# Two-block transformer kernel, dense passes: tokens and accumulator in twos of 16-token runs, upper runs first, at three address distances

## The chip, the core and the metric

The kernel runs on one core of a Trainium2 chip. The metric is device time of one execution in microseconds (us). All data are on the core: weights come from HBM once, and the tokens (512 of them, 1024 features) stay in SBUF from the first load to the last store.

## The reference

`reference()` puts a sequence of 512 tokens through two blocks, in float32:

- `first_block`: a norm, one projection to 18 groups of 128 columns, four mixers (gated MLP over chunks, RG-LRU, HGRN2, pooling), an output projection, a convolutional feed-forward network of width 2816, and an embedding gate.
- `second_block`: two hybrid layers. Each has this core (shortened):

```python
h = _rms(x) * norm1_g
proj = h @ w_in
aq, ak, av, rw, rq, rk, rv, rg, gates = _split(proj, IN_SIZES)
o_a = sliding_window_attention(aq, ak, av, sinks) @ w_attn_o
o_b = rwkv7_time_mix(rw, ...) @ w_rwkv_o
o_c = retention(rq, rk, rv, rg) @ w_ret_o
g = jax.nn.sigmoid(gates).reshape(B, T, N_BRANCH, D)
x = x + (g[:, :, 0] * o_a + g[:, :, 1] * o_b + g[:, :, 2] * o_c) @ w_out
h2 = _rms(x) * norm2_g
x = x + (jax.nn.silu(h2 @ w_ffn_gate) * (h2 @ w_ffn_up)) @ w_ffn_down
```

Most of the arithmetic is in the dense products of the 512 tokens with weight matrices.

## The kernel before, in words

**Layout.** Features lie on the 128 partitions and tokens along the free dimension. A tile such as `xg_hi` has 8 chunks (`DC`) of 512 tokens (`T`), so one chunk is 2048 bytes per partition.

**Dense products.** A float32 value is split into a high part that fits the fp32r format and a low part, the rest. A product takes three matmuls per chunk: high weights by high tokens, high weights by low tokens, low weights by high tokens. This text calls one such matmul, 128 x 128 weights by 512 tokens into one accumulator bank, a *dense pass*. The weights are the operand that is loaded into the array (LDWEIGHTS, shown as PEld), the tokens the operand that is streamed through it.

**Slots.** A slot makes 128 output features: 8 chunks and so 24 passes (4 chunks and 12 passes for the output projections of the mixers, 6 and 18 for the last part of the feed-forward products, 2 and 6 for the embedding). Two slots alternate, with accumulators `acc[0]` and `acc[1]`, weight tiles `w_hi[:, s]`, `w_lo[:, s]` and the raw weights in `raw[:, s]`. For each slot

- SyncE loads 512 KB (or less) of raw weights when the slot before in the same place has been split,
- GpSimd makes the high part (line 369, when the high passes of the slot before are done) and the low part (line 376, when all its passes are done),
- TensorE runs the passes, through `slot`, `late`, `three`, `part` or `first_slots`, all by the helper `mm` at line 550,
- VectorE or ScalarE takes the accumulator away.

The tokens of a product are in one of these pairs of tiles: `xg` (normed tokens, for the input, gate, feed-forward-up and output-gate products), `hid` (hidden or mixed features), `y` (mixer outputs of the first block), `y1` and `y2` (mixer outputs of the layers, placed over `z_rw` and `z_rt`), `emb` (embedding). `an_hi` and `an_lo`, sums over attention queries in the same number format, use `mm` and are not among the dense passes here.

**Order of work.** Each engine has a program written out by hand, and semaphores join them. In the RWKV part of a layer TensorE runs a chain of small matmuls that depends on VectorE, ScalarE and GpSimd at each step. Between the steps the list `FILLS` puts dense passes of later slots, 96 for each of 4 pairs of heads, in each of the 2 layers. The retention and attention parts put whole slots between their steps.

**Addresses.** `place` hands out SBUF addresses. With `line=` an address is moved up until it is that number modulo `LINE`, 512 bytes. Before the change every token tile has START, 128, and by the same rule `raw`; `w_hi` and `w_lo` follow `raw` directly at multiples of 512 bytes, so they are at 128 as well. A weight tile of one pass is 128 x 4 = 512 bytes per partition.

Of the kernel before, what the change touches and what calls it, by code (L numbers as in the profile page):

```python
# [14 lines left out]
F32, F32R, U32 = mybir.dt.float32, mybir.dt.float32r, mybir.dt.uint32  # L15
# [3 lines left out]
P = 128  # L19
T = 512  # L20
NT = T // P
D = 1024
DC = D // P
# [5 lines left out]
EPS = 1e-6  # L29
LN_EPS = 64e-5  # L30
DECAY = float(np.exp(-0.5))
LINE, START = 512, 128


B1_IN, X_OUT, O_PAIRS, PE_PAIRS = 9, 4, 24, 8
# [71 lines left out]
def build(nc, dram, out):  # L107
    ctx = ExitStack()
    with ctx:
# [3 lines left out]
        def place(name, shape, dt=F32, offset=None, line=None):  # L113
            n = 4 * int(np.prod(shape))
            if offset is None:
                if line is not None:
                    at[0] += (line - at[0]) % LINE
                offset = at[0]
                at[0] += (n + 31) // 32 * 32
            return nc.alloc_sbuf_tensor_at(name, [P, *shape], dt, offset=offset), offset  # L120

        x, _ = place("x", (DC, T))
        xg_hi, _ = place("xg_hi", (DC, T), F32R, line=START)
        xg_lo, _ = place("xg_lo", (DC, T), F32R, line=START)
        junk, _ = place("junk", (1,))
        raw, _ = place("raw", (2, DC * P), line=START)
        w_hi, _ = place("w_hi", (2, DC * P), F32R)
        w_lo, _ = place("w_lo", (2, DC * P), F32R)
        rstd, _ = place("rstd", (T,))
# [4 lines left out]
        base = at[0]  # L134
# [2 lines left out]
        for name, shape in FIRST:  # L137
            K[name], _ = place(name, shape, U32 if name == "hgmask" else F32)
        z, _ = place("z", (18, T))
        y_hi, _ = place("y_hi", (DC, T), F32R, line=START)  # L140
        y_lo, _ = place("y_lo", (DC, T), F32R, line=START)
        m1 = {}
        for name, shape in (("ta", (2, T)), ("tb", (2, T)), ("tc", (2, T)), ("td", (2, T + 16)), ("te", (2, T)), ("tf", (2, T)),
                            ("tg", (2, T)), ("th", (2, T))):
# [17 lines left out]
        for name, shape in RETAT:  # L162
            K[name], _ = place(name, shape)
        at[0] = max(end, at[0])
        z_rw, rw_at = place("z_rw", (14, T), line=START)
        z_rt, rt_at = place("z_rt", (16, T))
        scratch = at[0]
        C4 = 4 * 4 * T
# [5 lines left out]
        y2_lo, _ = place("y2_lo", (4, T), F32R, offset=rt_at + C4)  # L174
        hid_hi, _ = place("hid_hi", (DC, T), F32R, offset=rt_at)
        hid_lo, _ = place("hid_lo", (DC, T), F32R, offset=rt_at + 2 * C4)
        emb_at = base + 24 * 1024 + (START - base) % LINE
        emb_hi, _ = place("emb_hi", (2, T), F32R, offset=emb_at)
        emb_lo, _ = place("emb_lo", (2, T), F32R, offset=emb_at + C4 // 2)
        emb, _ = place("emb", (2, T), F32, offset=emb_at + C4)  # L180
        assert {a % LINE for a in (rw_at, rt_at, emb_at)} == {START} and emb_at + 3 * C4 // 2 <= rt_at and base + 4 * sum(int(np.prod(shape)) for _, shape in FIRST) <= emb_at

        rw = {}
        for name, shape in (("kk", (T,)), ("sq", (T,)), ("kp", (T,)), ("a", (T,)), ("Lr", (T,)), ("Dl", (T,)), ("eM", (T,)),
# [355 lines left out]
        def _(pe):  # L540
# [4 lines left out]
            def columns_of(w, s, k):  # L545

                return w[:, s, k * P:(k + 1) * P]

            def mm(o, a, b, first, last, shared=False):
                return nc.tensor.matmul(o, a, b, start=first, stop=last, skip_group_check=shared)  # L550

            def slot(s, I, a, chunks, early=False, stat=None, to=None, free=None):

                hi, lo = a
                if early:
                    pe.wait_ge(w_half[s], I + 1)
                else:
                    pe.wait_ge(w_split[s], I + 2)
                if to is None:
                    pe.wait_ge(acc_free[s], I + 1 if free is None else free)  # L560
                pe.sem_inc(pe_turn, 1)
                n = len(chunks)
                o = acc[s] if to is None else to
                for m, v in ((0, hi), (0, lo), (1, hi)):
                    w = (w_hi, w_lo)[m]
                    if early and m == 1:
                        pe.wait_ge(w_split[s], I + 2)
                        pe.sem_inc(pe_turn, 1)
                    for k, c in enumerate(chunks):
                        last = mm(o[:], columns_of(w, s, k), v[:, c, :], v is hi and m == 0 and k == 0, m == 1 and k == n - 1)  # L570
                    if v is lo:
                        last.then_inc(hi_done[s], 1)
                        if stat is not None:
                            pe.wait_ge(keep_in, load_wait * len(keep_names))
                            stats(stat)
                last.then_inc(slot_done[s], 1)

            def late(s, I, a, chunks, ready, count, order=None, early=False, stat=None):

                pe.wait_ge(w_half[s], I + 1) if early else pe.wait_ge(w_split[s], I + 2)  # L580
                pe.wait_ge(acc_free[s], I + 1)
                pe.sem_inc(pe_turn, 1)
                n = len(chunks)
                if early:
                    for k, c in enumerate(chunks[:-1]):
                        pe.wait_ge(ready, count + k + 1)
                        pe.sem_inc(pe_turn, 1)
                        mm(acc[s][:], columns_of(w_hi, s, k), a[0][:, c, :], k == 0, False)
                        mm(acc[s][:], columns_of(w_hi, s, k), a[1][:, c, :], False, False)
                    pe.wait_ge(w_split[s], I + 2)  # L590
                    pe.sem_inc(pe_turn, 1)
                    for k, c in enumerate(chunks[:-1]):
                        mm(acc[s][:], columns_of(w_lo, s, k), a[0][:, c, :], False, False)
                    if stat is not None:
                        stats(stat)
                    pe.wait_ge(ready, count + n)
                    pe.sem_inc(pe_turn, 1)
                    k, c = n - 1, chunks[-1]
                    mm(acc[s][:], columns_of(w_hi, s, k), a[0][:, c, :], False, False)
                    mm(acc[s][:], columns_of(w_hi, s, k), a[1][:, c, :], False, False).then_inc(hi_done[s], 1)  # L600
                    mm(acc[s][:], columns_of(w_lo, s, k), a[0][:, c, :], False, True).then_inc(slot_done[s], 1)
                    return
                for i, k in enumerate(order or range(n)):
                    c = chunks[k]
                    pe.wait_ge(ready, count + i + 1)
                    pe.sem_inc(pe_turn, 1)
                    mm(acc[s][:], columns_of(w_hi, s, k), a[0][:, c, :], i == 0, False)
                    last_hi = mm(acc[s][:], columns_of(w_hi, s, k), a[1][:, c, :], False, False)
                    last = mm(acc[s][:], columns_of(w_lo, s, k), a[0][:, c, :], False, i == n - 1)
                last_hi.then_inc(hi_done[s], 1)  # L610
                last.then_inc(slot_done[s], 1)

# [6 lines left out]

            def three(s, a, k, first, last):  # L620

                mm(acc[s][:], columns_of(w_hi, s, k), a[0][:, k, :], first, False)
                hi_pass = mm(acc[s][:], columns_of(w_hi, s, k), a[1][:, k, :], False, False)
                return hi_pass, mm(acc[s][:], columns_of(w_lo, s, k), a[0][:, k, :], False, last)

            def hid_slots(I, n, count, ahead=0):
                if not ahead:
# [187 lines left out]
            pe.wait_ge(acc_free[0], I + 1)  # L815
            for c in full:
                w = columns_of(w_hi, 0, c)
                mm(acc[0][:], w, xg_hi[:, c, :], c == 0, False)
                last = mm(acc[0][:], w, xg_lo[:, c, :], False, False)
            last.then_inc(hi_done[0], 1)  # L820
            pe.wait_ge(w_split[0], I + 2)
            for c in full:
                last = mm(acc[0][:], columns_of(w_lo, 0, c), xg_hi[:, c, :], False, c == DC - 1)
                if c < DC - 1:
                    last.then_inc(xg_free, 1)
            last.then_inc(slot_done[0], 1)
# [2 lines left out]
            def first_slots(I):  # L829
# [1 line left out]
                early, rest = range(6), range(6, DC)  # L831

                def one(s, w, v, c, first=False, last=False):
                    return mm(acc[s][:], columns_of(w, s, c), v[:, c, :], first, last, True)

                def started(s):
                    pe.wait_ge(w_half[s], I + 1)
# [31 lines left out]
            for l in range(LAYERS):  # L869
# [7 lines left out]
                def part(s, I, lo, hi):  # L877

                    for k in range(lo, hi):
                        if k == 0:  # L880
                            pe.wait_ge(w_half[s], I + 1)
                            pe.sem_inc(pe_turn, 1)
                            pe.wait_ge(acc_free[s], I + 1)
                            pe.sem_inc(pe_turn, 1)
                        if k == 2 * DC:
                            pe.wait_ge(w_split[s], I + 2)
                            pe.sem_inc(pe_turn, 1)
                        w, v, c = (w_hi, w_hi, w_lo)[k // DC], (xg_hi, xg_lo, xg_hi)[k // DC], k % DC
                        last = mm(acc[s][:], columns_of(w, s, c), v[:, c, :], k == 0, k == 3 * DC - 1, True)
                        if k == 2 * DC - 1:  # L890
                            last.then_inc(hi_done[s], 1)
                        if k == 3 * DC - 1:
                            last.then_inc(slot_done[s], 1)
# [1849 lines left out]
```

## Time and profile before

| what | us |
|---|---|
| median of 3 runs | 2546.61 |
| lowest and highest run | 2546.43, 2551.27 |
| the profiled execution, its own time | 2548.05 |
| span of that execution, first to last instruction | 2546.2 |
| TensorE busy in it | 2511.3 |
| GpSimd busy in it | 1512.5 |
| VectorE busy in it | 1311.4 |
| ScalarE busy in it | 691.6 |

The durations quoted below come from the one profiled execution. Its own time is 1.8 us more than its span, which is what lies ahead of the first instruction and behind the last. In the profile PE is TensorE with its matmuls, PEld its weight loads, DVE VectorE, ACT ScalarE, POOL GpSimd and SP SyncE. A matmul's record runs from its start to its modelled end; since matmuls follow each other through the array, records of neighbours overlap, and from one start to the next is less time than one record lasts. L550 is line 550 of the kernel.

### The profile page before, as it was taken

Reading aid. Unit: us, or ns where it says so; the run is one execution under the profiler, and the core shown is the slowest. Engines: PE = TensorE matmul, PEld = TensorE weight load, DVE = VectorE, ACT = ScalarE, POOL = GpSimd, SP = SyncE. Lnnn points to the kernel's source line nnn. Section 1 sums busy time; section 2 is a strip of 40 time slices with the busy share of each in tenths; the row PEclk is TensorE's granted clock in tenths of the full one; section 3 lists DMA queues with packets and bytes.
Section 4 is the critical chain, followed back from the end, with each engine's and each line's share of the span. In section 5 each row is a group of like instructions: output and inputs, shape, how many; then the busy total and the mean of one; then the engine's idle time right before and its main releaser. Section 6 shows DMA issues by size and latency. Waiting matters only on the chain.

```text
span 2546.2 us, 47105 instructions
## 1 busy us (share of the span) xinstructions
PE 2511.3 (99%) x16344; PEld 2012.3 (79%) x16344; DVE 1311.4 (52%) x1979; ACT 691.6 (27%) x1290; POOL 1512.5 (59%) x963
## 2 busy tenths in 40 slices
PE   8989999999999999999999999999999999999999
PEld 6868888887877778888888888867678888888887
DVE  7867555465566657663322224566647663322224
ACT  4452000024135446521100002134446531100002
POOL 5666666656646455556666666645454556666665
PEclk9999999999999999999999999999999999999999
DMA  4213222223211122223222223211122223222223
GB/s 167 71 43 119 91 99 99 91 86 117 92 51 52 44 97 69 72 87 103 93 97 99 96 93 122 91 47 50 51 97 67 75 87 103 91 99 95 95 99 99
DMA packets 72442, 222.55 MB, mean 87 GB/s; under 512 B 9312, under 2 KB 12256, under 8 KB 72288
## 3 DMA queue, kind: packets, MB, share of 16 engines
q1 hardware_dynamic: 71856, 220.36, 26.3%
q8 instruction: 96, 1.57, 0.3%
q14 instruction: 58, 0.48, 0.1%
q10 hardware_dynamic: 432, 0.14, 0.0%
HBM read 218.37 MB, written 2.10 MB: 87 GB/s over the span
## 4 chain that ended last, share of the span: by engine, by line
PE 92%; DVE 4%; DVEq 1%; issue 1%; DMA 1%; POOL 1%; ACT 0%; ACTq 0%; POOLq 0%; SPq 0%
PE acc L550 80%; PE bank L550 10%; DMA raw<-in_w_pg 1%; PE bank L1214 0%; POOL w_lo L376 0%; DVE sumsq L1252 0%; DVE y_lo L1252 0%; DVE bank L1252 0%; DVE xg_lo L1345 0%; POOL w_hi L369 0%; DVE bank L1611 0%; DMA vec<-in_vec 0%; DVE att L1464 0%; DVEq L1412 0%; DVEq L1709 0%
## 5 line engine op out<-in xcount | busy, mean ns | idle before, releaser
L376 POOL TENSOR_TENSOR w_lo<-raw,w_hi 128x1024 fp32r<-128x1024 f32 (+3 forms) x438 | 961.8, 2196 | 301.3 <-PE acc L550 242.1
L369 POOL TENSOR_SCALAR w_hi<-raw 128x1024 fp32r<-128x1024 f32 (+3 forms) x438 | 438.2, 1000 | 584.1 <-PE acc L550 503.1
L550 PE MATMUL acc<-xg_hi,w_hi 128*128 128x512 f32 x2208 | 581.8, 397 | 6.7 <-DVE xg_lo L1345 2.9
L550 PE MATMUL acc<-xg_lo,w_hi 128*128 128x512 f32 x2208 | 568.8, 393 | 0.0
L550 PE MATMUL acc<-xg_hi,w_lo 128*128 128x512 f32 x2208 | 562.7, 393 | 0.2 <-POOL w_lo L376 0.2
L550 PEld LDWEIGHTS acc<-xg_hi,w_hi 128*128 128x128 f32 x2208 | 408.6, 188 | 107.1 <-issue 20.9
L550 PEld LDWEIGHTS acc<-xg_hi,w_lo 128*128 128x128 f32 x2208 | 411.3, 188 | 88.4 <-issue 1.5
L550 PEld LDWEIGHTS acc<-xg_lo,w_hi 128*128 128x128 f32 x2208 | 411.2, 188 | 87.4 <-issue 1.5
L2131 ACT ACTIVATE ffn_act<-ffn_t 128x512 f32<-128x512 f32 x100 | 63.2, 632 | 742.6 <-DVEq L1312 600.7
L1252 DVE TENSOR_TENSOR x<-x,acc 128x512 f32<-128x512 f32 x104 | 71.3, 686 | 311.1 <-PE acc L550 310.6
L1252 DVE TENSOR_TENSOR bank<-acc,rstd 128x512 f32<-128x512 f32 x72 | 50.3, 699 | 263.4 <-PE acc L550 263.3
L550 PE MATMUL acc<-hid_hi,w_hi 128*128 128x512 f32 x656 | 178.1, 390 | 0.6
L550 PE MATMUL acc<-hid_lo,w_hi 128*128 128x512 f32 x656 | 177.6, 389 | 0.0
L550 PE MATMUL acc<-hid_hi,w_lo 128*128 128x512 f32 x656 | 170.5, 389 | 0.0
L1252 DVE TENSOR_TENSOR ffn_t<-acc,rstd 128x512 f32<-128x512 f32 x100 | 69.2, 692 | 196.1 <-PE acc L550 181.6
L550 PEld LDWEIGHTS acc<-hid_hi,w_hi 128*128 128x128 f32 x656 | 123.1, 188 | 28.1 <-DVE hid_lo L1252 1.6
L550 PEld LDWEIGHTS acc<-hid_hi,w_lo 128*128 128x128 f32 x656 | 123.1, 188 | 25.6
L550 PEld LDWEIGHTS acc<-hid_lo,w_hi 128*128 128x128 f32 x656 | 123.1, 188 | 25.4
L2148 ACT ACT_TABLE_LOAD x95 | 121.9, 1283 | 9.4 <-DMA bs<-in_bs 5.1
L2131 ACT ACTIVATE ffn_act<-bank 128x512 f32<-128x512 f32 x22 | 13.2, 599 | 306.2 <-DVEq L1612 306.2
L550 PE MATMUL acc<-y_hi,w_hi 128*128 128x512 f32 x256 | 73.1, 406 | 7.0 <-DVEq L1562 4.8
L2131 ACT ACTIVATE bank<-x,gains 128x512 f32<-128x512 f32 x56 | 38.6, 690 | 143.1 <-DVEq L1285 95.2
(351 smaller groups left out, 2708.4 us busy)
## 6 DMA issues: line engine op xcount, KB each, us to landing
raw<-in_w_up SPq DMA_DIRECT2D x132, 512.0 KB, 3.2
raw<-in_w_down SPq DMA_DIRECT2D x48, 512.0 KB, 3.2
raw<-in_w_gate SPq DMA_DIRECT2D x48, 512.0 KB, 3.2
raw<-in_w_ret SPq DMA_DIRECT2D x32, 512.0 KB, 3.3
raw<-in_w_rw SPq DMA_DIRECT2D x28, 512.0 KB, 3.2
raw<-in_w_o SPq DMA_DIRECT2D x48, 256.0 KB, 2.7
raw<-in_w_in SPq DMA_DIRECT2D x18, 512.0 KB, 3.2
raw<-in_w_down SPq DMA_DIRECT2D x24, 384.0 KB, 3.0
```

The costliest lines, as they stand in the source:

```text
L369: nc.gpsimd.tensor_scalar(w_hi[:, s, 0:n], raw[:, s, 0:n], 1.0, 0.0, ALU.mult, ALU.add).then_inc(w_half[s], 1)
L376: nc.gpsimd.tensor_tensor(w_lo[:, s, 0:n], raw[:, s, 0:n], bits(w_hi[:, s, 0:n]), ALU.subtract).then_inc(w_split[s], 1)
L550: return nc.tensor.matmul(o, a, b, start=first, stop=last, skip_group_check=shared)
L1252: return v.tensor_tensor(o, a, b, op)
L2131: return nc.scalar.activation(o, i, f, **kw)
L2148: nc.scalar.preload_act_table_set(name)
```

## The change

Nothing is added to or taken from the list of instructions. Two things change.

First, the order in which a dense pass reads its 512 tokens and writes its 512 accumulator columns. Before, both go from column 0 to column 511. After, the 512 columns (2048 bytes) are seen as two halves of 1024 bytes with 16 runs of 16 columns (64 bytes) each. A pass takes run 15 of the lower half, run 15 of the upper half, run 14 of each, and so on down to run 0 of each; within a run the columns go up. Tokens and accumulator are walked in the same order, so every value lands where it did.

Second, the addresses. The weights stay at 128 modulo 512. The token tiles move: `xg` and `emb` to 256 (128 bytes from the weights), `y` to 192 (64 bytes), `z_rw` to 320 and with it `z_rt`, `y1`, `y2` and `hid` (192 bytes). Before, all these distances are 0.

```diff
-LINE, START = 512, 128
+LINE = 512
+RUN = 16
...
-        xg_hi, _ = place("xg_hi", (DC, T), F32R, line=START)
-        xg_lo, _ = place("xg_lo", (DC, T), F32R, line=START)
+        xg_hi, _ = place("xg_hi", (DC, T), F32R, line=256)
+        xg_lo, _ = place("xg_lo", (DC, T), F32R, line=256)
...
-        raw, _ = place("raw", (2, DC * P), line=START)
+        raw, _ = place("raw", (2, DC * P), line=128)
...
-        y_hi, _ = place("y_hi", (DC, T), F32R, line=START)
-        y_lo, _ = place("y_lo", (DC, T), F32R, line=START)
+        y_hi, _ = place("y_hi", (DC, T), F32R, line=192)
+        y_lo, _ = place("y_lo", (DC, T), F32R, line=192)
...
-        z_rw, rw_at = place("z_rw", (14, T), line=START)
+        z_rw, rw_at = place("z_rw", (14, T), line=320)
...
-        emb_at = base + 24 * 1024 + (START - base) % LINE
+        emb_at = base + 24 * 1024 + (256 - base) % LINE
...
+            def blocks_down(ap):
+
+                return ap.rearrange("p (h r c) -> p r h c", h=2, c=RUN)[:, ::-1]
+
+            def dense(o, a, b, first, last, shared=False):
+
+                return mm(blocks_down(o), a, blocks_down(b), first, last, shared)
+
...
-                        last = mm(o[:], columns_of(w, s, k), v[:, c, :], v is hi and m == 0 and k == 0, m == 1 and k == n - 1)
+                        last = dense(o[:], columns_of(w, s, k), v[:, c, :], v is hi and m == 0 and k == 0, m == 1 and k == n - 1)
```

The last pair of lines is from `slot`. `late`, `three`, `part`, `first_slots` and the last embedding slot call `dense` in place of `mm` in the same way, so that all dense passes have the new order. The fp32 sums, transposes and the small matmuls of the mixers keep `mm`.

## Rows read from the trace of the kernel before

**Rows 1.** The page: span, busy time, share and instructions of each engine.

```profile
span 2546.2 us, 47105 instructions
...
PE 2511.3 (99%) x16344; PEld 2012.3 (79%) x16344; DVE 1311.4 (52%) x1979; ACT 691.6 (27%) x1290; POOL 1512.5 (59%) x963
```

**Rows 2.** The page, chain of waits that ended last: shares by engine, by line.

```profile
PE 92%; DVE 4%; DVEq 1%; issue 1%; DMA 1%; POOL 1%; ACT 0%; ACTq 0%; POOLq 0%; SPq 0%
PE acc L550 80%; PE bank L550 10%; DMA raw<-in_w_pg 1%; PE bank L1214 0%; POOL w_lo L376 0%; DVE sumsq L1252 0%; DVE y_lo L1252 0%; DVE bank L1252 0%; DVE xg_lo L1345 0%; POOL w_hi L369 0%; DVE bank L1611 0%; DMA vec<-in_vec 0%; DVE att L1464 0%; DVEq L1412 0%; DVEq L1709 0%
```

**Rows 3.** Groups by line, engine, form; one dense row of each three.

```profile
line engine op names shapes xcount | busy us, mean ns | idle before us <-releasers
L550 PE MATMUL acc<-xg_hi,w_hi 128*128 128x512 f32 x2208 | 581.8, 397 | 6.7 <-DVE xg_lo L1345 2.9 <-issue 1.6 <-POOL w_hi L369 1.2
...
L550 PE MATMUL acc<-hid_hi,w_hi 128*128 128x512 f32 x656 | 178.1, 390 | 0.6
...
L550 PE MATMUL acc<-y_hi,w_hi 128*128 128x512 f32 x256 | 73.1, 406 | 7.0 <-DVEq L1562 4.8 <-DVE y_lo L1252 2.2
...
L550 PE MATMUL acc<-emb_hi,w_hi 128*128 128x512 f32 x16 | 4.9, 389 | 0.0
...
L550 PE MATMUL bank<-xg_hi,w_hi 128*128 128x512 f32 x16 | 4.0, 389 | 0.0
```

**Rows 4.** Timeline of TensorE, a feed-forward stretch; first and seventeenth of its groups.

```profile
start us, us, engine line op out<-in xcount [idle before <-releaser]
1281.06 1.98 PE L550 MATMUL acc<-xg_lo,w_hi 128*128 128x512 f32 x8
...
1310.08 1.98 PE L550 MATMUL acc<-xg_hi,w_lo 128*128 128x512 f32 x8
```

**Rows 5.** Three stretches: busy time of each engine, granted clock, DMA share.

```profile
core 0: us, PE busy (x) PEld busy (x) DVE busy (x) ACT busy (x) POOL busy (x), PEclk, DMA share, GB/s
12.60:15.20 2.60, 2.58 (x6) 2.14 (x7) 2.48 (x5) 1.41 (x3) 0.00 (x0) 0.50 0.06 24
440.00:480.00 40.00, 40.00 (x178) 33.14 (x177) 8.64 (x12) 0.60 (x1) 25.66 (x15) 1.00 0.30 103
700.00:900.00 200.00, 195.40 (x3163) 141.71 (x3161) 121.07 (x233) 83.93 (x193) 105.02 (x67) 1.00 0.14 47
```

**Rows 6.** Timeline of TensorE from the first passes on.

```profile
9.70 0.47 PE L550 MATMUL acc<-xg_hi,w_hi 128*128 128x512 f32 x1 [1.99 <-DVE xg_lo L1345]
10.01 0.39 PE L550 MATMUL acc<-xg_lo,w_hi 128*128 128x512 f32 x1
...
13.18 0.63 PE L550 MATMUL acc<-xg_lo,w_hi 128*128 128x512 f32 x1
...
14.89 0.54 PE L550 MATMUL acc<-xg_hi,w_lo 128*128 128x512 f32 x1
...
15.49 0.40 PE L550 MATMUL acc<-xg_lo,w_hi 128*128 128x512 f32 x1
...
16.42 0.40 PE L550 MATMUL acc<-xg_hi,w_lo 128*128 128x512 f32 x1
...
18.35 2.00 PE L550 MATMUL acc<-xg_hi,w_hi 128*128 128x512 f32 x8
20.19 1.98 PE L550 MATMUL acc<-xg_lo,w_hi 128*128 128x512 f32 x8
```

**Rows 7.** Timeline of TensorE: two fp32 sums and what follows.

```profile
1004.02 1.02 PE L550 MATMUL bank<-rt_sq,headones 128*128 128x512 f32 x2
1004.88 0.60 PE L1141 MATMUL bank<-ident,z_rt 128*128 128x128 f32 x4
```

**Rows 8.** Timeline of the weight loads (PEld), the first passes.

```profile
9.67 0.19 PEld L550 LDWEIGHTS acc<-xg_hi,w_hi 128*128 128x128 f32 x1 [3.53 <-issue]
9.78 0.19 PEld L550 LDWEIGHTS acc<-xg_lo,w_hi 128*128 128x128 f32 x1
10.01 0.19 PEld L550 LDWEIGHTS acc<-xg_hi,w_lo 128*128 128x128 f32 x1
```

**Rows 9.** Groups by form: fp32 reads of two 64-column runs (rw_AR), one run (rw_AW).

```profile
L550 PE MATMUL bank<-rw_AR,rw_eM 64*64 64x128 f32 x256 | 8.8, 275 | 0.7 <-DVEq L1709 0.7
L550 PE MATMUL bank<-rw_AW,rw_G 64*64 64x128 f32 x256 | 8.8, 275 | 1.2 <-ACT rw_G L2131 1.2
```

**Rows 10.** What TensorE waited for, the three longest in total.

```profile
engine line waited for: us in total, times, longest us
PE acc L550 <- DVEq L1562: 4.8, 1, 4.8
PE bank L550 <- issue: 4.1, 5, 1.3
PE bank L550 <- DVEq L1709: 3.3, 6, 0.9
```

**Rows 11.** The page, costliest groups: the split of the weights on GpSimd.

```profile
L376 POOL TENSOR_TENSOR w_lo<-raw,w_hi 128x1024 fp32r<-128x1024 f32 (+3 forms) x438 | 961.8, 2196 | 301.3 <-PE acc L550 242.1
L369 POOL TENSOR_SCALAR w_hi<-raw 128x1024 fp32r<-128x1024 f32 (+3 forms) x438 | 438.2, 1000 | 584.1 <-PE acc L550 503.1
```

More of the change, by code:

```diff
@@ L180, in build @@
         emb, _ = place("emb", (2, T), F32, offset=emb_at + C4)
-        assert {a % LINE for a in (rw_at, rt_at, emb_at)} == {START} and emb_at + 3 * C4 // 2 <= rt_at and base + 4 * sum(int(np.prod(shape)) for _, shape in FIRST) <= emb_at
+        assert emb_at + 3 * C4 // 2 <= rt_at and base + 4 * sum(int(np.prod(shape)) for _, shape in FIRST) <= emb_at
         rw = {}
@@ L587, in late @@
                         pe.sem_inc(pe_turn, 1)
-                        mm(acc[s][:], columns_of(w_hi, s, k), a[0][:, c, :], k == 0, False)
-                        mm(acc[s][:], columns_of(w_hi, s, k), a[1][:, c, :], False, False)
+                        dense(acc[s][:], columns_of(w_hi, s, k), a[0][:, c, :], k == 0, False)
+                        dense(acc[s][:], columns_of(w_hi, s, k), a[1][:, c, :], False, False)
                     pe.wait_ge(w_split[s], I + 2)
@@ L592, in late @@
                     for k, c in enumerate(chunks[:-1]):
-                        mm(acc[s][:], columns_of(w_lo, s, k), a[0][:, c, :], False, False)
+                        dense(acc[s][:], columns_of(w_lo, s, k), a[0][:, c, :], False, False)
                     if stat is not None:
@@ L598, in late @@
                     k, c = n - 1, chunks[-1]
-                    mm(acc[s][:], columns_of(w_hi, s, k), a[0][:, c, :], False, False)
-                    mm(acc[s][:], columns_of(w_hi, s, k), a[1][:, c, :], False, False).then_inc(hi_done[s], 1)
-                    mm(acc[s][:], columns_of(w_lo, s, k), a[0][:, c, :], False, True).then_inc(slot_done[s], 1)
+                    dense(acc[s][:], columns_of(w_hi, s, k), a[0][:, c, :], False, False)
+                    dense(acc[s][:], columns_of(w_hi, s, k), a[1][:, c, :], False, False).then_inc(hi_done[s], 1)
+                    dense(acc[s][:], columns_of(w_lo, s, k), a[0][:, c, :], False, True).then_inc(slot_done[s], 1)
                     return
@@ L606, in late @@
                     pe.sem_inc(pe_turn, 1)
-                    mm(acc[s][:], columns_of(w_hi, s, k), a[0][:, c, :], i == 0, False)
-                    last_hi = mm(acc[s][:], columns_of(w_hi, s, k), a[1][:, c, :], False, False)
-                    last = mm(acc[s][:], columns_of(w_lo, s, k), a[0][:, c, :], False, i == n - 1)
+                    dense(acc[s][:], columns_of(w_hi, s, k), a[0][:, c, :], i == 0, False)
+                    last_hi = dense(acc[s][:], columns_of(w_hi, s, k), a[1][:, c, :], False, False)
+                    last = dense(acc[s][:], columns_of(w_lo, s, k), a[0][:, c, :], False, i == n - 1)
                 last_hi.then_inc(hi_done[s], 1)
@@ L620, in three @@
             def three(s, a, k, first, last):
-                mm(acc[s][:], columns_of(w_hi, s, k), a[0][:, k, :], first, False)
-                hi_pass = mm(acc[s][:], columns_of(w_hi, s, k), a[1][:, k, :], False, False)
-                return hi_pass, mm(acc[s][:], columns_of(w_lo, s, k), a[0][:, k, :], False, last)
+                dense(acc[s][:], columns_of(w_hi, s, k), a[0][:, k, :], first, False)
+                hi_pass = dense(acc[s][:], columns_of(w_hi, s, k), a[1][:, k, :], False, False)
+                return hi_pass, dense(acc[s][:], columns_of(w_lo, s, k), a[0][:, k, :], False, last)
             def hid_slots(I, n, count, ahead=0):
@@ L817, in _ @@
                 w = columns_of(w_hi, 0, c)
-                mm(acc[0][:], w, xg_hi[:, c, :], c == 0, False)
-                last = mm(acc[0][:], w, xg_lo[:, c, :], False, False)
+                dense(acc[0][:], w, xg_hi[:, c, :], c == 0, False)
+                last = dense(acc[0][:], w, xg_lo[:, c, :], False, False)
             last.then_inc(hi_done[0], 1)
@@ L822, in _ @@
             for c in full:
-                last = mm(acc[0][:], columns_of(w_lo, 0, c), xg_hi[:, c, :], False, c == DC - 1)
+                last = dense(acc[0][:], columns_of(w_lo, 0, c), xg_hi[:, c, :], False, c == DC - 1)
                 if c < DC - 1:
@@ L833, in one @@
                 def one(s, w, v, c, first=False, last=False):
-                    return mm(acc[s][:], columns_of(w, s, c), v[:, c, :], first, last, True)
+                    return dense(acc[s][:], columns_of(w, s, c), v[:, c, :], first, last, True)
                 def started(s):
@@ L888, in part @@
                         w, v, c = (w_hi, w_hi, w_lo)[k // DC], (xg_hi, xg_lo, xg_hi)[k // DC], k % DC
-                        last = mm(acc[s][:], columns_of(w, s, c), v[:, c, :], k == 0, k == 3 * DC - 1, True)
+                        last = dense(acc[s][:], columns_of(w, s, c), v[:, c, :], k == 0, k == 3 * DC - 1, True)
                         if k == 2 * DC - 1:
```

## The prediction

> **What bounds the kernel now.** I read the header and the busy shares first: TensorE is busy for 2511.3 of 2546.2 us, and the next engine, GpSimd, for 59% [rows 1]. The chain of waits agrees: 92% of it is TensorE, 80% matmuls into acc, at the one helper line 550 [rows 2]. Among the groups by form, the dense passes are 512-column fp32r matmuls: three groups each of 2208 (xg), 656 (hid), 256 (y) and 16 (emb, and xg into a spare bank) [rows 3]. Together that is 3 x (2208 + 656 + 256 + 16 + 16) = 9456 passes, and the change touches all of them.
>
> The mean of 390 ns in those groups is not what a pass costs, because passes overlap. The cost is the pitch, from start to start. In a settled stretch sixteen groups of eight start from 1281.06 to 1310.08 us: 29.02 us / 128 = 226.7 ns [rows 4]. Passes at this pitch make 9456 x 226.7 ns = 2144 us, 84% of the span.
>
> Is 226.7 ns what 512 columns need? Three groups of rows say no.
> - At the start the granted clock is 0.50, that is 1.2 GHz [rows 5]. There four passes start from 13.18 to 14.89 us, a pitch of 427 ns [rows 6], just 512 columns at 1.2 GHz. At full clock twice that speed would be 213.5 ns; the settled pitch is 13.2 ns more. So the excess does not scale with TensorE's clock: it appears only when the array asks for columns at 2.4 GHz.
> - The plain fp32 sums over 512 columns start 0.43 us apart at full clock [rows 7]. If such a sum goes over its columns twice, which its double time suggests, one trip takes 215 ns.
> - After an idle gap the pitch is irregular: from 15.49 to 16.42 us four passes take 0.93 us, 232.5 ns each, and by 18.35 to 20.19 eight take 230 each [rows 6], before it settles at 226.7. A fixed cost per pass would not wander. This looks like two streams that meet at places that depend on their phase.
>
> The second stream is at hand. A weight load starts with every pass and lasts 0.19 us [rows 8]. After an idle gap the first load starts at 9.67 and the second at 9.78 [rows 8], and the first pass takes 0.47 instead of 0.39 us [rows 6], so it waited for its weights: I estimate that 128 weights per partition (512 bytes) are read in about 0.11 us. That is 14 ns per 64 bytes. Tokens are read at 512 columns in 226.7 ns, or 7.1 ns per 64 bytes. My reading is that weight load and moving tokens collide in SBUF, and the pass pays about 12 ns for it.
>
> **The change part by part.**
>
> *Order of reading.* No instruction is added or removed; every dense pass reads 64 bytes from the lower 1024 bytes of its row or from the upper, alternately, and then steps 64 bytes down. Two runs take 2 x 7.1 = 14.2 ns, which is the time in which the weight load covers 64 bytes. If places 1024 bytes apart count as the same, and if weights are read from the top down, tokens and weights now keep a constant distance and need not meet. Whether weights are read downwards no row shows.
>
> Price if they no longer meet: between 213.5 ns (half of the cold pitch) and 226.7 ns (nothing gained). I take the fp32 trip, 215 ns, since it is the one row at full clock with a weight load beside it. Gain: 11.7 ns x 9456 = 110.6 us. The bound of 213.5 gives 13.2 x 9456 = 124.8 us.
>
> The Trainium skill, "TensorE: Matmul & The Clock Gate", section "Wait — 56ns, not 53.3ns?", gives 215.7 ns for a warm back-to-back matmul of 512 columns; by it the gain would be 11.0 x 9456 = 104 us. This kernel's fp32r passes do not reach that figure; its fp32 trips do.
>
> *Cost of the order itself.* 32 runs per pass mean 32 jumps, in the read and in the accumulator write. The nearest rows are the fp32 reads of two 64-column runs against one run of 128 columns: 275 and 275 ns [rows 9]. That prices a jump at 0. It is one jump, on the read side alone, in fp32. The other bound is one period of 2.4 GHz per jump: 32 x 0.417 = 13.3 ns per pass, 126 us. I take 0, as the row has it.
>
> *The three distances.* All weights start at 128 modulo 512 before and after. By the placements xg and emb move to distance 128 (3 x (2208 + 16 + 16) = 6720 passes), hid, y1 and y2 to 192 (1968 + 576), and block 1's y to 64 (192 passes). Every dense row of before is at distance 0, so no row prices a distance. I take all as clear; the bound on the other side is that a distance gains nothing.
>
> *What no longer hides.* In the RWKV stretch TensorE already has gaps: 195.4 of 200 us busy [rows 5]. Dense passes fill its waits there, 96 per head pair, 4 pairs, 2 layers: 768 passes, so 9.0 us of gain is at stake. Waits of TensorE are short there (DVE, 3.3 us over 6 times [rows 10]), so I let half turn into waits: 4.5 us back, between 0 and 9. Elsewhere GpSimd splits a weight slot in 1.0 + 2.2 us [rows 11]; for a pair of slots 6.4 us, against 48 passes of TensorE, 10.9 us now and 10.3 then. That cover stays; were it gone, each slot would wait for GpSimd. In a dense stretch DMA is 30% busy [rows 5], and weights still arrive early.
>
> *Sum.* 2548.05 us (the profiled execution, span 2546.2) - 110.6 + 4.5 = 2442; the median of the runs is 1.4 us below that execution, so 2441 us. Irregular pitches would go too, worth perhaps another 5 us, which I leave in the range.
>
> **The rivals.**
>
> *A. All distances clear:* 2441, between 2420 (213.5 ns, irregular passes too) and 2465 (pitch 217.5 and all fills lost). For it: the cold pitch and the irregular pitch. Against: the direction of the weight read is a guess. Chance 0.42.
>
> *B. One distance clears, others still meet.* If only 192 clears: 2544 x 11.7 = 30 us, 2517. If only 128: 6720 x 11.7 = 79 us, 2468. Phase can also leave part of a collision everywhere. Between 2465 and 2540; chance 0.20.
>
> *C. Nothing changes.* The excess is not a collision, or meetings are only moved about: 2546.6; chance 0.08. A rule speaks for it: the Trainium skill, "SBUF — State Buffer", section "Who interferes with whom", gives TensorE two independent read ports, one for the moving operand and one for the weights, and says that it never waits on anyone. The pitch that is 13.2 ns over the clock's share only at 2.4 GHz, and wanders, speaks against it.
>
> *D. Slower: the jumps cost.* Read or accumulator write loses time at each of the 32 jumps of a pass. At one period of 2.4 GHz it is +126 us: 2562 if the collisions go as well (2546.6 + 126 - 111), 2673 if they stay. It decides from 11.7 / 32 = 0.37 ns per jump upwards. For it: [rows 9] test one jump, not 32, and no row has an accumulator written in runs. Against: 64 bytes are long runs, and fp32 shows nothing. Chance 0.30. A rule speaks for it: the Trainium skill, "PSUM — Partial Sum Buffer", section "Specifications (TRN2)", says "any non-contiguous AP slows matmuls significantly", and gives 8-byte lines there; runs of 64 bytes would fill such lines, so its letter is against this change and its reason is not. No row shows a dense pass with such an output.
>
> **How the numbers follow.** The likeliest is A, 2441 us. Below 2420 I leave 0.03. A, B and C lie under 2552; of D I include the part in which the jumps eat little more than the gain, up to 2600, about half, which leaves 0.15 above. So the range is 2420 to 2600, and A's own is 2420 to 2465. About 0.2% (5 us) is what a measurement of this kernel tells from no change. Faster by more: A and B, 0.62. Within: C, 0.08. Slower: D, 0.30.
>
> **What would show it.** Pass pitch decides, by tile: eight starts in about 1.72 us instead of 1.81, in xg (distance 128), hid (192) and block 1's y (64) separately. The cold pitch should stay 427 ns and the weight load 0.19 us. Under A the irregular pitches after gaps vanish. In the RWKV stretch TensorE's waits for DVE grow by some us. GpSimd's share rises by the ratio of the spans. Under D the pitch is above 226.7 in every tile alike, in the cold stretch perhaps too; under B tiles differ. I would be wrong if the weights are read upwards, if the meeting place does not repeat within 1024 bytes, or if a jump costs.

## The result, and the profile after

The changed kernel takes 2556.58 us (median of 8 runs, 2554.64 to 2559.06) against 2546.82 us for the kernel before (8 runs, 2545.19 to 2551.27). The ratio is 1.0036, with a 95% interval from 1.0026 to 1.0047: slower by 0.36%, 9.8 us. The prediction of 2441 us was wrong, in its sign too; only the wide range, 2420 to 2600 us, held the time.

The page of the changed kernel first: span, busy time of each engine, and the chain of waits by line. (Line 551 is the helper that was line 550.)

```profile
span 2556.8 us, 47105 instructions
...
PE 2520.8 (99%) x16344; PEld 2010.2 (79%) x16344; DVE 1309.8 (51%) x1979; ACT 690.8 (27%) x1290; POOL 1502.3 (59%) x963
...
PE acc L551 80%; PE bank L551 10%; DMA raw<-in_w_pg 1%; PE bank L1223 0%; POOL w_lo L377 0%; DVE sumsq L1261 0%; DVE y_lo L1261 0%; DMA vec<-in_vec 0%; POOL w_hi L370 0%; DVE bank L1620 0%; DVE att L1473 0%; DVE bank L1261 0%; DVEq L1421 0%; DVEq L1718 0%; DVE xg_lo L1354 0%
```

Against [rows 1, 2] TensorE has 9.5 us more busy time and the span is 10.6 us longer, with the same number of instructions and the same chain. GpSimd's busy time fell by 10.2 us; it has next to no share of the chain, and why it fell is open. Taken pass by pass against the trace of before, the time from one dense pass's start to the next makes up the loss: 6.0 us in xg, 4.0 us in hid, 0.7 us in y, and all the rest 0.1 us less. So the time is in the pitch of the dense passes. Two rows of the timeline of TensorE show it for xg (distance 128), sixteen groups of eight apart, as in [rows 4]:

```profile
1280.00 1.99 PE L551 MATMUL acc<-xg_hi,w_hi 128*128 128x512 f32 x8
...
1309.22 1.99 PE L551 MATMUL acc<-xg_lo,w_hi 128*128 128x512 f32 x8
```

29.22 us / 128 = 228.3 ns, where it was 226.7. In hid (distance 192) there are two kinds of stretch. The first two rows are from block 1, the next two from the first layer, and the last two, in groups of six, from the end of the same layer:

```profile
441.20 2.06 PE L551 MATMUL acc<-hid_hi,w_hi 128*128 128x512 f32 x8
...
448.77 2.06 PE L551 MATMUL acc<-hid_lo,w_hi 128*128 128x512 f32 x8
...
1323.81 1.97 PE L551 MATMUL acc<-hid_hi,w_hi 128*128 128x512 f32 x8
...
1334.69 1.97 PE L551 MATMUL acc<-hid_hi,w_hi 128*128 128x512 f32 x8
...
1567.65 1.58 PE L551 MATMUL acc<-hid_hi,w_hi 128*128 128x512 f32 x6
...
1590.37 1.58 PE L551 MATMUL acc<-hid_lo,w_hi 128*128 128x512 f32 x6
```

In block 1 it is 7.57 us / 32 = 236.6 ns; in the layer first 10.88 us / 48 = 226.7 ns, exactly as before, and at its end 22.72 us / 96 = 236.7 ns. Same tile, same distance, same order, two lasting pitches. Three stretches of hid are at the slow one, 411 passes in all: each is slow from its first passes after an interruption to its end. At the same place in the second layer the pass before the interruption starts 505 ns ahead of the next, against 510 ns in the first, and the stretch settles at 226.7. So how a stretch begins seems to decide; what in the beginning does is not shown.

This gives the loss its parts. The three slow stretches of hid cost 411 x 10 ns = 4.1 us, an estimate that agrees with the 4.0 us measured. xg loses 1.6 ns in each pass of its settled stretches, but 6720 x 1.6 ns = 11 us would be too much: in stretches of under 24 passes between interruptions (some 2000 passes, those of the RWKV part among them) the loss is only 0.4 us, and the first passes took 0.8 us less, since the granted clock was 1.00 there in this profiled execution and 0.50 in that of before [rows 5].

The RWKV stretch, as in the last of [rows 5] (columns: length, then busy time of PE, PEld, DVE, ACT, POOL, granted clock, DMA share, GB/s):

```profile
700.00:900.00 200.00, 194.82 (x3147) 142.64 (x3147) 121.64 (x232) 83.81 (x193) 104.50 (x67) 1.00 0.15 48
```

194.8 us busy where it was 195.4. The two RWKV parts, from their first small matmul to their last, are 0.4 and 1.6 us shorter than before: as good as unchanged.

### The profile page after: what moved, and what is told of

It is laid out like the page before. It is cut to its first block, busy times and chain, and to the rows that moved or that the text cites. A ratio compares the mean times of both kernels' runs of the same rounds, so it can differ in the third digit from the quotient of the medians.

```text
span 2556.8 us, 47105 instructions
## 1 busy us (share of the span) xinstructions
PE 2520.8 (99%) x16344; PEld 2010.2 (79%) x16344; DVE 1309.8 (51%) x1979; ACT 690.8 (27%) x1290; POOL 1502.3 (59%) x963
## 4 chain that ended last, share of the span: by engine, by line
PE 91%; DVE 4%; DVEq 1%; issue 1%; DMA 1%; POOL 1%; ACT 0%; ACTq 0%; POOLq 0%; SPq 0%
PE acc L551 80%; PE bank L551 10%; DMA raw<-in_w_pg 1%; PE bank L1223 0%; POOL w_lo L377 0%; DVE sumsq L1261 0%; DVE y_lo L1261 0%; DMA vec<-in_vec 0%; POOL w_hi L370 0%; DVE bank L1620 0%; DVE att L1473 0%; DVE bank L1261 0%; DVEq L1421 0%; DVEq L1718 0%; DVE xg_lo L1354 0%
```

## The experiments

The theories: 1, the excess of a pass over 213.3 ns is a meeting of the token read with the weight read; 2, the new order costs by its jumps; 3, leaving distance 0 costs. Theories 4 to 8 came up on the way. Theory 5 is that order and distance together set the settled pitch and that jumps are free; the others are explained in the expectations that name them. In the texts a pitch is called settled when it is the mean over the last 24 starts of a stream.

### The two halves of the change, each alone

Order alone: the changed kernel with all tiles back at distance 0.

```diff
-        xg_hi, _ = place("xg_hi", (DC, T), F32R, line=256)
+        xg_hi, _ = place("xg_hi", (DC, T), F32R, line=128)
```

(the same for `xg_lo`, `y`, `z_rw` and `emb`)

> The changed kernel with all token tiles back at distance 0 from the weights; only the new order stays. Theory 1 (the passes pay for meetings of token reads and weight reads; order and distance set where they meet): the settled pitch is neither that of before (226.7 ns) nor that of the changed kernel in xg (228.5), since at distance 0 tokens and weights now step down side by side; 230 to 240 ns would be 2580 to 2670 us. Theory 2 (the new order costs time by itself, at its jumps, and distance is nothing): the same mean pitch as the changed kernel, 228.6 ns in every tile, about 2556 us. Theory 3 (leaving distance 0 costs the time, the order is nothing): 226.7 ns, 2547 us.

Distances alone: the changed kernel with the old order.

```diff
-                return mm(blocks_down(o), a, blocks_down(b), first, last, shared)
+                return mm(o, a, b, first, last, shared)
```

> The kernel before with the three distances alone; columns go up from 0 to 511 again. Theory 1: pitch differs by tile (xg at 128, hid at 192), each at its own value between 224 and 236 ns; 2535 to 2600 us. Theory 2 (the order costs): 226.7 ns in every tile, 2547 us. Theory 3 (the distances cost): 228.5 in xg and 228.8 in hid as in the changed kernel, about 2556 us.

Order alone: 2581.85 us against 2548.05, ratio 1.0136 (1.0120 to 1.0151). Distances alone: 2593.36 us, ratio 1.0179 (1.0165 to 1.0192). Two rows of each timeline of TensorE, xg, ten groups of eight apart; order alone first:

```profile
1291.08 2.00 PE L551 MATMUL acc<-xg_lo,w_hi 128*128 128x512 f32 x8
...
1309.48 2.00 PE L551 MATMUL acc<-xg_hi,w_lo 128*128 128x512 f32 x8
```

And distances alone:

```profile
1290.18 2.02 PE L551 MATMUL acc<-xg_hi,w_lo 128*128 128x512 f32 x8
...
1308.76 2.03 PE L551 MATMUL acc<-xg_hi,w_hi 128*128 128x512 f32 x8
```

18.40 us / 80 = 230.0 ns and 18.58 us / 80 = 232.3 ns. Each half by itself costs several times what the whole costs. So neither theory 2 nor theory 3 holds: order and distance act together, and the change is two losses that nearly cancel. Both times lie in the ranges of theory 1.

### Bare streams: four orders at eight distances

> This kernel leaves out the whole model: it loads tokens and weights and runs bare streams of 48 fp32r passes, with no other engine at work, in four orders (up, down, twos down as in the change, twos up) at eight distances (0 to 448 bytes in steps of 64) from the weights. Theory 1: the settled pitch depends on order and distance together; up at distance 0 gives 226.7, twos down at 128 gives 228.5, and some pair reaches about 215 ns. Theory 2 (fixed excess plus jumps): up and down give 226.7 at every distance, both orders of twos 228.6 at every distance. Theory 3: up at 0 alone gives 226.7, and every order at another distance 228 to 229.

The core of this kernel, in which no other engine works:

```python
def stream(o, b, order, n):
    for k in range(n):
        nc.tensor.matmul(order(o[:]), w[:, (k % 8) * P:(k % 8 + 1) * P], order(b[:, k % 4, :]),
                         start=k == 0, stop=k == n - 1)
```

Its timeline of TensorE; `toka`, `tokb`, ... lie at distance 0, 64, ... Each row is one stream of 48 passes, and its pitch is the next row's start less its own, by 48. Each of these kernels of bare streams ran once; streams that stand in several of them agree to 0.1 ns when settled.

```profile
29.93 11.04 PE L78 MATMUL up<-toka,w 128*128 128x512 f32 x48
40.81 11.17 PE L78 MATMUL up<-tokb,w 128*128 128x512 f32 x48
51.81 11.32 PE L78 MATMUL up<-tokc,w 128*128 128x512 f32 x48
62.97 11.36 PE L78 MATMUL up<-tokd,w 128*128 128x512 f32 x48
74.17 11.06 PE L78 MATMUL up<-toke,w 128*128 128x512 f32 x48
...
208.04 11.36 PE L78 MATMUL twosdown<-toka,w 128*128 128x512 f32 x48
219.24 11.12 PE L78 MATMUL twosdown<-tokb,w 128*128 128x512 f32 x48
230.20 11.14 PE L78 MATMUL twosdown<-tokc,w 128*128 128x512 f32 x48
241.19 11.06 PE L78 MATMUL twosdown<-tokd,w 128*128 128x512 f32 x48
252.08 11.36 PE L78 MATMUL twosdown<-toke,w 128*128 128x512 f32 x48
```

Up at 0, 64, 128, 192: 226.7, 229.2, 232.5, 233.3 ns. Twos down: 233.3, 228.3, 229.0, 226.9. The ends of these streams, when they have settled, give 226.7, 228.9, 232.3, 233.3 and 233.3, 228.3, 228.3, 226.7 (means over the last 24 starts). At 256 to 448 bytes the same values come again. Down is 233.3 and twos up 240.0 at every distance. None of the 32 is below 226.7, so the pair at about 215 ns that theory 1 asked for is not there.

The kernels' pitches are in this table: before (up, 0) 226.7; distances alone (up, 128) 232.3; the changed kernel (twos down) 228.3 in xg and 226.7 in most of hid. Order alone (twos down, 0) is at 230.0 in most stretches of xg in the kernel, and at 233.3, the pitch found here, in stretches with about a quarter of the passes: two lasting pitches again, as in hid. Distances alone wanders between 231.7 and 233.3 in the stretches of xg.

### Bare streams: is it the weight read?

> This kernel leaves out the whole model: bare streams of 48 passes, columns up, distance 0, one thing changed in each: weights of 96, 64 and 32 columns; one weight column read 128 times; every pass a start of its own; two accumulators in turn; the same weights each time; the same tokens each time; weights two elements apart; distances of 32 and 96 bytes; 384 and 256 token columns; fp32 in place of fp32r. Theory 1 (meetings with the weight read): the excess over 213.3 ns shrinks with the weight columns, from 13.3 ns at 128 to about 10, 7 and 3 at 96, 64 and 32 columns. Theory 2 (a fixed cost of an fp32r pass, whatever the weight load does): 226.7 ns at every number of weight columns. Theory 4 (the accumulator: reading and writing back the sums costs it): starts of their own or two accumulators in turn change the pitch, weight columns do not.

Its timeline of TensorE. The first row merges the four streams with 128, 96, 64 and 32 weight columns, the third the two with 384 and 256 token columns; the last is fp32.

```profile
25.58 44.24 PE L88 MATMUL base<-tok,w 128*128 128x512 f32 x192
69.67 11.29 PE L88 MATMUL weightstill<-tok,w 128*128 128x512 f32 x48
...
157.93 14.26 PE L88 MATMUL other<-tok,w 128*128 128x384 f32 x96
172.02 20.77 PE L88 MATMUL other<-x,raw 128*128 128x512 f32 x48
```

44.09 us / 192 = 229.6 ns: fewer weight columns make the passes slower than the 226.7 ns of 128 columns, not faster. Theory 1 asked for a fall to 216 at 32 columns; the settled values are 230.0, 230.0 and 231.7 ns at 96, 64 and 32. They are not the constant 226.7 of theory 2 either. The two shorter passes take 14.09 us / 96 = 146.8 ns on average. Their columns alone are (160.0 + 106.7) / 2 = 133.3 ns at 2.4 GHz, so the excess is 13.5 ns, as it is for 512 columns (13.3): it is paid once per pass, not per column. A start in every pass, two accumulators in turn, the same weights, or the same tokens each time leave 226.7, so theory 4 falls too. The other streams show that the way in which the weights are read still matters: one weight column read 128 times (the second row) takes 231.7 ns, weights two elements apart 233.3, and distances of 32 and 96 bytes 233.3 each.

> This kernel leaves out the whole model: bare streams as before, distance 0 unless said. Weights of 1 column that start 0, 32, ... 224 bytes further (eight streams), of 32 columns at 0, 64, 128, 192; tokens read 512 times from one place, with 128 weight columns and with 1; blocks of 64, 32 and 16 columns from the upper down; the two halves swapped; tokens two elements apart; bfloat16 tokens and weights. Theory 1 (the excess comes from the weight read): with 1 weight column the pitch falls to 214 to 217 ns wherever that column lies. Theory 6 (the excess is in the pass's own read of fp32r tokens and its start, and the weight read only shifts the phase): with 1 column it stays at 226 or more, and it falls only where the tokens are read from one place, or are bfloat16. Blocks of 64 columns and halves show whether jumps cost anything: they keep the order modulo 256 bytes, so 226.7 if jumps are free (Theory 5), more by a fixed amount per jump under Theory 2.

Again the timeline of TensorE, 48 passes to a row (the last row has lost one record):

```profile
43.37 11.26 PE L74 MATMUL few<-t_one_a,w 128*1 128x512 f32 x48
54.46 11.26 PE L74 MATMUL few<-t_one_b,w 128*1 128x512 f32 x48
...
176.55 10.66 PE L74 MATMUL acc<-t_still,w 128*128 128x512 f32 x48
187.05 10.65 PE L74 MATMUL few<-t_still_one,w 128*1 128x512 f32 x48
197.54 11.09 PE L74 MATMUL acc<-t_blocks_sixtyfour,w 128*128 128x512 f32 x48
208.47 11.35 PE L74 MATMUL acc<-t_blocks_thirtytwo,w 128*128 128x512 f32 x48
...
230.86 11.07 PE L74 MATMUL acc<-t_halves,w 128*128 128x512 f32 x48
241.77 21.91 PE L74 MATMUL acc<-t_skip,w 128*128 128x512 f32 x48
263.75 10.31 PE L74 MATMUL acc<-t_bf,wb 128*128 128x512 bf16 x47
```

With one weight column the pitch settles at 231.1 ns, at all eight places of that column, though the weight load now lasts 83 ns instead of 188: theory 1 falls. With all 512 tokens read from one place it is 20.99 us / 96 = 218.6 ns over the two rows, with 128 weight columns and with 1 alike: 8 ns of the excess go when the token read stays in place, and none when the weights shrink. Tokens two elements apart settle at 453.3 ns, twice 226.7 for the same 512 columns. So 8 of the 13.3 ns belong to the token read. The other 5.3 ns stay with the tokens in one place, and no run shows what they are; every stream has a weight load in each pass, so a fixed cost of a pass is not ruled out for them. bfloat16 settles at 215.8 ns, but there tokens and weights both have half the bytes (the weight load lasts 98 ns), so this stream does not tell which of the two, or the number format, counts.

Blocks of 64 columns from the upper down (227.7 with its first passes, 226.7 settled) and the swapped halves (227.3, settled 226.7) cost nothing: they keep the order modulo 256 bytes. Blocks of 32 do not: modulo 256 bytes they are columns up at distance 128, which took 232.3, and they take 233.1.

### Read or write?

> This kernel leaves out the whole model: bare streams at token distances 0, 64, 128, 192. Twos down on the token read alone, on the accumulator write alone, and on both; twos up on each alone; both with 1 weight column; up, and twos down on both, with the weights moved 64 bytes up. Theory 6 (it is the read of the tokens): read alone gives the table of both (233.3, 228.3, 228.3, 226.7), write alone gives that of up (226.7, 228.9, 232.3, 233.3). Theory 8 (it is the accumulator write): the other way round. With the weights moved, the tables shift by one place if the distance between tokens and weights decides, and stay where they are if the tokens' own address modulo 256 does; with 1 weight column the four distances come to one value if weights matter only through their own reads.

Timeline of TensorE, twos down on the read alone (`read`), then on the write alone (`write`), then up with the weights moved 64 bytes up:

```profile
89.13 11.36 PE L81 MATMUL acc<-t_read_ata,w 128*128 128x512 f32 x48
100.33 11.12 PE L81 MATMUL acc<-t_read_atb,w 128*128 128x512 f32 x48
111.29 11.14 PE L81 MATMUL acc<-t_read_atc,w 128*128 128x512 f32 x48
122.27 11.06 PE L81 MATMUL acc<-t_read_atd,w 128*128 128x512 f32 x48
133.17 11.07 PE L81 MATMUL acc<-t_write_ata,w 128*128 128x512 f32 x48
144.08 11.17 PE L81 MATMUL acc<-t_write_atb,w 128*128 128x512 f32 x48
...
311.82 11.35 PE L81 MATMUL acc<-t_up_moved_ata,w 128*128 128x512 f32 x48
323.01 11.09 PE L81 MATMUL acc<-t_up_moved_atb,w 128*128 128x512 f32 x48
333.93 11.17 PE L81 MATMUL acc<-t_up_moved_atc,w 128*128 128x512 f32 x48
```

Read alone: 233.3, 228.3, 228.8, 227.1, the table of twos down. Write alone: 227.3 at 0, settled 226.7, 228.9, 232.3, 233.3 at the four distances, the table of up. The order of the accumulator costs nothing that can be measured, so the whole difference between the orders is in the token read, as theory 6 had it, and theory 8 falls. With the weights moved, up gives 233.1 for tokens at 128 modulo 512 and 227.5 for those at 192: the table has shifted by one place, so with 128 weight columns the distance decides and not the tokens' own address. With one weight column, twos down gives 230.0, 231.1, 228.3 and 228.3 (settled), between the values that distance makes with 128. That is not the one value that was expected if weights matter only through their own reads; whether distance or the tokens' own address makes these four differ was not separated. The weights thus have a part: where they lie moves the pitch between 226.7 and 233.3 ns, but with nearly all of their read gone the passes still take more than 226.7.

### Can any order beat 226.7?

> This kernel leaves out the whole model: bare streams of 48 passes with 128 weight columns, twenty more orders of the 512 tokens at distances 0, 64, 128 and 192: fours and eights of 16-token runs (up and down), twos and fours of 32-token runs, twos of 8- and 4-token runs, every second or fourth run first, neighbouring runs swapped, short runs from the upper down. Theory 6 (the excess is in the pass's own read of fp32r tokens; the order modulo 256 bytes sets it, the weight read only shifts the phase): every order lies between 218.6 ns (one place) and some 240 to 250, most above 226.7; if an order with fewer changes of place exists that comes below 226.7, it would be among the fours and eights of 16. Theory 7 (226.7 is a floor for any order that walks through its tokens): none of the 80 streams falls below 226.7 ns.

Eighty more streams, timeline of TensorE, the best order found:

```profile
844.06 11.06 PE L95 MATMUL acc<-t_swapped_wide_atc,w 128*128 128x512 f32 x48
854.96 11.17 PE L95 MATMUL acc<-t_swapped_wide_atd,w 128*128 128x512 f32 x48
```

Swapping neighbouring runs of 32 columns, at distance 128: 10.90 us / 48 = 227.1, settled 226.7, level with before. All others lie between 228.9 and 266.7 (runs of 8 swapped). Theory 7 holds for what was tried. The best order is not a new one: modulo 256 bytes it is columns up at distance 0. In the same sense its rows at distances 192, 64 and 0 are columns up at 64, 192 and 128, and they take 228.9, 233.3 and 233.3 ns against 228.9, 233.3 and 232.3 there: the rule holds within 0.1 ns in three of four cases and misses by 1 ns in one.

### Back in the kernel

All tiles at 192, where twos down settles at 226.7 in the bare streams:

```diff
-        xg_hi, _ = place("xg_hi", (DC, T), F32R, line=256)
+        xg_hi, _ = place("xg_hi", (DC, T), F32R, line=320)
```

(the same for `xg_lo`, `y` and `emb`)

> The changed kernel with every token tile at distance 192 (xg, emb and y too). In the bare streams twos down settles at 228.3 ns at distances 64 and 128 and at 226.7 at 192. Theory 5 (order and distance together set the settled pitch, by the table of the bare streams; the change loses at 128): xg settles at 226.7, and the kernel comes back to 2547 to 2556 us, the upper end if xg gets irregular stretches as hid has in the changed kernel (mean 228.8). Theory 2 (the jumps of the new order cost): no change from the changed kernel, about 2556 us.

2556.96 us, ratio 1.0040 (1.0027 to 1.0052). Timeline of TensorE, xg, ten groups apart:

```profile
1291.39 1.98 PE L551 MATMUL acc<-xg_lo,w_hi 128*128 128x512 f32 x8
...
1309.52 1.98 PE L551 MATMUL acc<-xg_hi,w_lo 128*128 128x512 f32 x8
```

18.13 us / 80 = 226.6: the settled pitch is that of before, as the table says. The time does not come back all the same; the profiled span is 2553.6, 7.4 us over that of before. Another stretch of xg in the same timeline, sixteen groups apart, shows why:

```profile
670.04 2.06 PE L551 MATMUL acc<-xg_hi,w_hi 128*128 128x512 f32 x8
...
700.33 2.06 PE L551 MATMUL acc<-xg_lo,w_hi 128*128 128x512 f32 x8
```

30.29 us / 128 = 236.6 ns: the second lasting pitch of hid, now in xg. This stretch has 167 passes and nothing between them, and runs at 236.6 from just after the small matmuls ahead of it to its end. In all, 18 stretches of eight or more passes of xg, hid and y do so, 831 passes in sum; at 10 ns each over 226.7 that is an estimated 8.3 us, enough for the loss; the long feed-forward stretches of xg lose nothing. So the table of the bare streams has the settled pitch right and leaves out the second one. The time is 1 us above the range of Theory 5 and the same as Theory 2 had it, but a pitch of 226.6 ns in xg is against Theory 2's reason.

And a downward order that is the same modulo 256 bytes, at distance 0:

```diff
-                return ap.rearrange("p (h r c) -> p r h c", h=2, c=RUN)[:, ::-1]
+                return ap.rearrange("p (r c) -> p r c", c=4 * RUN)[:, ::-1]
```

> The kernel before (distance 0), with the tokens and the accumulator of every dense pass in eight blocks of 64 columns from the upper down, up within a block: a downward order with jumps that keeps the order modulo 256 bytes. Theory 5 (the settled pitch goes by the order modulo 256 bytes, jumps are free): 226.7 ns and 2547 us, no change from before. Theory 2 (jumps cost, and the change lost 1.3 ns per pass to 32 of them): a quarter of the jumps, 227 ns, 2549 to 2550 us; if it is the downward direction that costs, 228.5 ns and 2556 us or more.

2549.09 us against 2548.11, ratio 1.0003 (0.9994 to 1.0012). Timeline of TensorE, xg, ten groups apart:

```profile
1290.85 1.98 PE L551 MATMUL acc<-xg_hi,w_hi 128*128 128x512 f32 x8
...
1308.98 1.98 PE L551 MATMUL acc<-xg_lo,w_hi 128*128 128x512 f32 x8
```

18.13 us / 80 = 226.6, the same to the tenth of a microsecond in its span (2546.2). Going down block by block, and jumping between blocks of 64 columns, is free. No run points to a version that beats the kernel before.

## Why the prediction was wrong

- **What bounds the kernel, 9456 passes at their pitch:** right. The kernels' times followed the pitch of the passes.
- **"My reading is that weight load and moving tokens collide in SBUF, and the pass pays about 12 ns for it": the step that failed.** The excess was real (13.3 ns), and it vanishes at half the clock [rows 6], but one weight column instead of 128 does not lower it: 231.1 ns. With one weight column and with 128, 8 of the 13.3 ns go when the token read stays in one place (218.6 ns); the other 5.3 are unexplained. The excess is paid once per pass, and the estimate of 0.11 us for the read of 128 weights held: a load of 128 columns lasts 188 ns, one of a single column 83. The irregular pitch that I took for two streams meeting is there with one weight column as well (226, 234, 234 ns in turn).
- **The price of 215 ns**, 110.6 us of gain, fell with it. It came from the fp32 sums by the guess that 0.43 us is two trips over the columns. In the bare streams an fp32 product shows as two matmuls of 429 ns each; whether 429 ns is two trips over the 512 columns or one at half the rate no run shows, so it was no price for an fp32r pass. No order or distance that walks through its tokens reaches 215 ns.
- **"I take all [distances] as clear":** wrong in the direction as well. Distance 0 was the best place for the old order, and the new order at 128 is at 228.3. This is rival C's "meetings are only moved about", which had a chance of 0.08 and was priced at no change; the streams and the kernel give 1.6 ns in the settled passes of xg and 10 ns in three stretches of hid.
- **The range** held 2556.58 us by luck: no rival had this mechanism. Order alone costs 34 us and distances alone 45 us, and it was not foreseen that together they would come to 10.
- **Cost of the jumps, 0:** right, shown by blocks of 64 for the read and by the write alone for 32 jumps in the accumulator. Rival D had the sign but not the mechanism. For the accumulator the Trainium skill, "PSUM — Partial Sum Buffer", section "Specifications (TRN2)", has any non-contiguous pattern slow a matmul; writing in runs of 16 columns left the pitch at 226.7 ns, so for runs of that length the measurement differs.
- **Two read ports.** The Trainium skill, "SBUF — State Buffer", section "Who interferes with whom", has the weight read independent of the token read. The streams agree in that 1 and 128 weight columns take the same 218.6 ns with the tokens in one place, and differ in that moving the weights by 64 bytes moves the pitch from 226.7 to 233.3 ns.
- **RWKV passes hidden:** right for a loss, and more than the half that was assumed. In distances alone, where an xg pass takes 5.6 ns more, the two RWKV parts are 1.2 and 0.7 us shorter than before. A gain was not there to be tested.
- **Other signs:** GpSimd's share was to change by the ratio of the spans alone, but its busy time fell from 1512.5 to 1502.3 us, which is open. The cold pitch could not be compared, since the changed kernel's profiled execution has a granted clock of 1.00 where that of before had 0.50.

Open: what loses the 13.3 ns once per pass, 8 of them in the token read; how the place of the weights comes in; and why some stretches last at 236.6 ns where others settle at 226.7. What was varied (order, distance, width of the weights, accumulator) shows where it is, not what it is.

## What to carry to other kernels

Before pricing the removal of an excess, make a bare stream that takes away the suspected cause alone: one run with one weight column would have told that the excess does not need the weights. When a pitch depends on a phase, halves of a change need not add: here +1.4% and +1.8% make +0.4%. A settled pitch in a bare stream is not yet a kernel's time: the same stretch can last at another pitch, and one stream shows only one of them. Look at the pitch stretch by stretch before putting a loss down to gaps.

## What the runs showed of the hardware that was not expected

- The pitch of fp32r passes with 128 weight columns depends on the order of the token read modulo 256 bytes and on the distance to the weights modulo 256 bytes: 226.7 to 266.7 ns for the same work.
- An fp32r pass takes 13.3 ns over its columns at 2.4 GHz at best, for each of three numbers of them: 226.7, 173.3 and 120.0 ns for 512, 384 and 256 columns.
- The order in which the accumulator is written, and jumps in the read that keep the order modulo 256 bytes, cost nothing measurable (226.7 ns each).
- The same order and distance can run at two lasting pitches: twos down at 192 at 226.7 and 236.6 ns, at 0 at 230.0 and 233.3. Every stretch of over 100 passes of the kernel before, columns up at distance 0, settles at 226.7.
